# Seven of the first block's eight output-projection units in a seven-product form, behind one plain unit

## The chip, the cores and the metric

The kernel runs on one core of one Trainium2 chip. The metric is the device time of one execution in microseconds (us), lower is better. The engines are TensorE (PE, with its weight loads shown as PEld), VectorE (DVE), ScalarE (ACT), GpSimd (POOL) and the DMA queues, of which SyncE (SP) issues the stream of weights.

## What is computed

Three blocks run one after the other over 256 tokens of width 1024, all in float32. The change is in the end of the first block, a hybrid of retention and a gated linear recurrence:

```python
proj = jnp.einsum('btd,de->bte', xn, w_in)
q, k, v, g_ret, x_lru, g_lru = jnp.split(proj, IN_SPLITS, axis=-1)
q = rotary(q...); k = rotary(k...) * RET_HEAD_DIM ** -0.5
o_ret = group_norm_heads(chunkwise_retention(q, k, v))
y_ret = o_ret * jax.nn.silu(g_ret)
xc = causal_depthwise_conv(x_lru, conv_w, conv_b)
o_lru = rg_lru(xc, gate_a_w, gate_a_b, gate_x_w, gate_x_b, lru_lambda)
y_lru = o_lru * jax.nn.silu(g_lru)
mixed = jnp.concatenate([y_ret, y_lru], axis=-1)      # 256 x 2048
h = h + jnp.einsum('bte,ed->btd', mixed, w_out)       # w_out: 2048 x 1024
return rms_norm(h, norm_out_g)
```

The second block (block attention, convolution, pooling, an FFN) and the third (FFNs, an RWKV mixer, a gated MLP mixer, cross attention) follow; they take its normed output.

## The kernel before

Activations are kept with the width on the 128 partitions and the 256 tokens in the free dimension; a tile of 8 blocks by 256 tokens holds one activation (`c.h`, `c.xn`, `c.work[0]` to `c.work[9]`). All weights come as one stream of 1 MB units. SP loads them in order into a ring of six slots (`c.ring`, the loop at L2909), each as soon as PE has finished the unit that held its slot six units earlier. The plan numbers the units: `b1_gret` and `b1_glru` (the two gates of block one) are units 16 to 23, `b1_out` (the output projection) is 24 to 31, `b2_q` begins at 32.

A plain unit of the output projection (`d_unit`, L302) holds 256 rows of `w_out` against all 1024 columns: 16 matmuls of 128x128 weights by 256 tokens, into the four PSUM banks 4 to 7. Each float32 matmul shows as two records in the trace. `b1_tensor` (L1034 to the end of the function) runs eight of them: units 0 to 3 read `y_ret` from `work[0]` as soon as its pair of blocks is written (`b1_y`), units 4 to 7 read `y_lru` from `work[7]` (`b1_y_lru`). The last unit completes the banks one after the other, and `add_residual` (L474) on DVE adds each to `c.h`, multiplies it by the gain of the next norm (`gain_blocks`) and folds in the squares that ACT makes. PE goes on with `norm_units` of `b2_q`, which takes the gained blocks one by one.

Other parts of the kernel already use a seven-product form of a 2x2 block product (`fast_products`, L593). A unit covers four pairs of blocks; it has 28 matmuls of 128x128 by 128, 56 records. It wants seven left sides, of which three are sums of weights that POOL writes beforehand (`prepare_weights`, L562: four additions over 128x512 for each unit, into one of two or three tiles, the additions of unit z waiting for PE to be done with the unit that had the same tile), and seven right sides, of which four are sums of activations (three DVE instructions for a pair of blocks in the FFN, L782 to L786). Its result comes as products in two banks, which `fast_sum` (L722) puts together: one ACT copy and four DVE additions. `p1` and `p2`, the first two products, need no sum of activations; the third, `p6`, does (`before_t`). In block one the q, k and v projections (`b1_fast`, ten units z = 0 to 9) have this form.

In `b1_vector` DVE is an in-order list. Its last part writes `y_ret` in four steps (`retention_out`, L1177 to L1182), `y_lru` in four (`lru_out`, L1198), and then runs `add_residual`. POOL's list is: the additions of `b1_fast`; the store of the attention bias of block two to DRAM (`bias_rows`, L2958, from eight partitions); a wait for that store and for the last use of the decay table (`b1_prob` 8, L2962); two loads of the skewed bias (L2964, L2965) into `c.table`, wanted by DVE in block two; the load of `mem` into `work[7]`, once `c.h` is complete.

Of the kernel before, what the change touches and what calls it, by code (L numbers as in the profile page):

```python
# [16 lines left out]
ALU = mybir.AluOpType  # L17
# [3 lines left out]
P = 128  # L21
T = 256
C = 1024
KB = C // P
UNITS = 6
# [27 lines left out]
PLAN = plan()  # L53
# [437 lines left out]


FAST = ["b2_ffn", "l0_ffn1", "l0_ffn2", "l1_ffn1", "l1_ffn2"]
FAST_ORDER = ["b1_fast", "b2_ffn", "l0_ffn1", "l0_x", "l0_ffn2", "l1_ffn1", "gm", "l1_x", "l1_ffn2"]
PREPS = 3


def fast_counts():

    unit_of, first_out, out = [], {}, 0  # L500
    first_unit_of = {}
    for name in FAST_ORDER:
        if name == "b1_fast":
            start, units, outs = PLAN["b1_q"][0] + 2, 10, 10
        elif name == "gm":
            start, units, outs = PLAN["gm_v"][0], 22, 18
        elif name in ("l0_x", "l1_x"):
            start, units, outs = PLAN[name + "q"][0] + 2, 6, 6
        else:
            start, units, outs = PLAN[name][0] + 2, 3 * FFI - 2, 2 * (FFI - 1) + 4  # L510
        first_unit_of[name], first_out[name] = len(unit_of), out
        unit_of += range(start, start + units)
        out += outs
    return unit_of, first_unit_of, first_out


FAST_UNIT, FAST_Z, FAST_G = fast_counts()
# [14 lines left out]
    return 2 if z < FAST_Z["b2_ffn"] else PREPS  # L532


def early_tile(c, z):

    if z % 2:
        flat = c.work[4][:, :, :].rearrange("p a b -> p (a b)")[:, 0:1536]
    else:
        flat = c.table[:, :, :].rearrange("p a b -> p (a b)")[:, 1536:3072]  # L540
    return flat.rearrange("p (s k n) -> p s k n", s=3, k=4)
# [247 lines left out]
def fast_residual(c, dve, name, f, scale, gain, ch):  # L789

    S, r = c.S, RESID.index(name)
    if name == "gm_out":
        g = FAST_G["gm"] + 14
    elif f is None:
        g = FAST_G[name[:-1]] + 2
    else:
        g = FAST_G[name] + 2 * (FFI - 1)

    def complete(b):
        if f is None and name != "gm_out":  # L800
            c.wait_done(dve, PLAN[name][0] + b)
        elif f is None:
            c.wait_done(dve, PLAN[name][0] + 2 * b + 1)
        elif b < 3:
            dve.wait_ge(S["bank_complete"], 3 * DPROJ.index(name) + b + 1)
        else:
            c.wait_done(dve, PLAN[name][0] + 3 * FFI - 1)

    for b in range(4):
        out = c.t1[:, b % 2, :]  # L810
        fast_sum(c, dve, g + b, out, lambda: complete(b), ch)
        dve.wait_ge(S["fast_read"], g + b + 1)
# [30 lines left out]
def b1_scalar(c, act):  # L843
# [27 lines left out]
    n0, q0 = PLAN["b1_q"]  # L871
# [40 lines left out]
    for p in range(5):  # L912
# [9 lines left out]
        if p < 4:  # L922
# [2 lines left out]
            act.wait_ge(S["b1_cen"], p + 1)  # L925
            nc.scalar.activation(c.t1[:, 1, :], W[0][:, 2 * p:2 * p + 2, :].rearrange("p a b -> p (a b)"),
                                 ACT.Square).then_inc(S["b1_cen_sq"], 1)
    rms_scalar(c, act, NK["b1_out"], 0)


def b1_tensor(c, pe):
# [100 lines left out]
    gate_unit(7, lambda: means(3))  # L1032
    variances(3)
    n0, _ = PLAN["b1_out"]  # L1034
    for u in range(8):
        pe.wait_ge(S["b1_y"] if u < 4 else S["b1_y_lru"], u % 4 + 1)
        src = W[0] if u < 4 else W[7]
        d_unit(c, pe, n0 + u, lambda k: src[:, 2 * (u % 4) + k, :], u == 0, u == 7,
               before_fourth=(lambda: pe.wait_ge(S["b1_var_read"], 4)) if u == 0 else None)


def b1_vector(c, dve, ch):
# [158 lines left out]
    for p in range(5):  # L1201
        if p < 4:
            for e in range(2):
                hd = 2 * p + e
                dve.wait_ge(S["b1_scores"], hd + 1)
                if hd == 4:
                    dve.wait_ge(S["decay_loaded"], 48)
                if p > 0:
                    dve.wait_ge(S["b1_o"], p)
                v.tensor_tensor(prob[:, e, 0:T + P], c.ps[:, 4 + e, 0:T + P], dec[:, hd, :], ALU.mult)\  # L1210
                    .then_inc(S["b1_prob"], 1)
            recurrence(p)
        gate(2 * p if p < 4 else 7)
        if p < 3:
            gate(2 * p + 1)
        if p < 4:
            dve.wait_ge(S["b1_mean"], p + 1)
            v.tensor_tensor(W[0][:, 2 * p:2 * p + 2, :].rearrange("p a b -> p (a b)"), c.t1[:, 0, :],
                            c.ps[:, 7, :], ALU.subtract).then_inc(S["b1_cen"], 1)
        if p > 0:  # L1220
            retention_out(p - 1)
        if p == 3:
            lru_out(0)
            lru_out(1)
    lru_out(2)
    lru_out(3)
    add_residual(c, dve, "b1_out", PLAN["b1_out"][0] + 7, 1.0, lambda b: ("norm_out_g", b))
    rms_vector(c, dve, "b1_out", c.h)


# [95 lines left out]

def b2_tensor(c, pe):
    S, nc, V, mm = c.S, c.nc, b2_views(c), c.nc.tensor.matmul
    norm_units(c, pe, "b2_q", "b1_out")

    pe.wait_ge(S["rstd_ready"], NK["b1_out"] + 1)
    for name in ("b2_k", "b2_v"):
        n0, q0 = PLAN[name]
        for u in range(2):
            p_unit(c, pe, n0 + u, q0 + u, c.h, token_major=name == "b2_v")
        if name == "b2_k":
            rms_tensor(c, pe, NK["mem"])
# [1552 lines left out]
def build(nc, x, params, consts, late_consts, stream, decay, gates, rel_bias, w_pool, bias_rows, mem, lora1,  # L2890
          lora_wa, lora_g, spatial, spatial_b, out):
    with ExitStack() as ctx:
# [56 lines left out]
        @block.gpsimd  # L2949
        def _(pool):  # L2950
            pool.dma_start(c.relb[0:32, :], rel_bias).then_inc(S["relb_loaded"], 16)
            pool.dma_start(c.wpool[:, :, :], w_pool).then_inc(S["relb_loaded"], 16)

            pool.wait_ge(S["b1_conv"], 6)
            prepare_weights(c, pool, "b1_fast")

            pool.wait_ge(S["b2_bias_read"], 1)
            pool.dma_start(bias_rows.rearrange("h p y -> h p y"),  # L2958
                           c.relg[0:8, :].rearrange("h (a y) -> h a y", a=1).to_broadcast([8, P, 384]))\
                .then_inc(S["bias_loaded"], 16)  # L2960
# [130 lines left out]
```

## Time and profile before

| | before |
|---|---|
| median of 3 runs | 2053.35 us (2051.73 to 2053.61) |
| the profiled execution | 2053.31 us |
| its span | 2051.5 us |
| PE busy | 2017.8 us, 98% of the span |
| PE weight loads busy | 1906.2 us, 93% |
| DVE busy | 1162.4 us, 57% |
| ACT busy | 377.3 us, 18% |
| POOL busy | 1071.3 us, 52% |
| granted TensorE clock, mean | 0.993 |

The span runs from the first to the last instruction; the execution around it adds 1.8 us. Busy time is the union of an engine's instructions. Starts are in us from the start of the span. The granted clock is a share of full speed (1.00 is 2.4 GHz, 0.50 is 1.2 GHz). In a timeline a row merges instructions of one kind that follow each other; "[idle before <-releaser]" stands where the engine had been idle.

### The profile page before, as it was taken

To read this page: it belongs to the slowest core of one execution; us is meant where nothing else is said; L and a number is where in the kernel's file an instruction comes from. 1 tells how busy PE (TensorE), PEld (TensorE's weight loads), DVE (VectorE), ACT (ScalarE), POOL (GpSimd) and SP (SyncE) were. 2 spreads that over 40 slices of the span, in tenths; PEclk is the share of its full clock that TensorE was granted. 3 is DMA by queue.
4 is the path that set the end of the run, shared out by engine and by line. 5 is a ranking of instruction groups with operands and counts; after the bars stand their busy time and mean duration, and the time that the engine had idled before them with its cause. 6 is when DMAs were issued, how large, how long until landed. Compare 5 with 4: busy or idle time off the path is not lost.

```text
span 2051.5 us, 39961 instructions
## 1 busy us (share of the span) xinstructions
PE 2017.8 (98%) x17174; PEld 1906.2 (93%) x17174; DVE 1162.4 (57%) x2002; ACT 377.3 (18%) x787; POOL 1071.3 (52%) x815
## 2 busy tenths in 40 slices
PE   8999999999999999999999999999999999999998
PEld 7998887899998999978788999999999999999998
DVE  6866134456516774436757577726772455576752
ACT  1352022133202000023421210001000231120000
POOL 1820000368853888300001568885888677547884
PEclk9999999999999999999999999999999999999999
DMA  8463443344443444523002344444444544434441
GB/s 313 149 187 138 164 162 114 125 165 168 175 173 123 165 167 172 180 103 123 24 4 103 116 155 173 175 165 164 165 165 166 204 163 147 151 115 167 171 175 64
DMA packets 44025, 307.67 MB, mean 150 GB/s; under 512 B 5304, under 2 KB 5560, under 8 KB 8016
## 3 DMA queue, kind: packets, MB, share of 16 engines
q1 hardware_dynamic: 40752, 291.78, 39.6%
q0 software_dynamic: 2096, 7.31, 1.3%
q10 hardware_dynamic: 1008, 6.10, 0.8%
q8 instruction: 135, 2.21, 0.4%
q14 instruction: 34, 0.28, 0.1%
HBM read 302.54 MB, written 2.62 MB: 149 GB/s over the span
## 4 chain that ended last, share of the span: by engine, by line
PE 91%; DVE 6%; issue 1%; ACT 1%; DMA 0%; DVEq 0%; SPq 0%; ACTq 0%
PE ps L612 60%; PE ps L252 13%; PE ps L311 5%; PE ps L249 2%; PE ps L271 1%; PE ps L286 1%; DVE sb_work L425 1%; PE ps L1730 1%; DVE sb_xn L2667 1%; DVE sb_work L418 1%; PE ps L1755 1%; PE ps L393 0%; DVE sb_h L813 0%; DMA sb_ring<-stream 0%; PE ps L2425 0%
## 5 line engine op out<-in xcount | busy, mean ns | idle before, releaser
L612 PE MATMUL ps<-sb_work,sb_ring 128*128 128x128 f32 x4064 | 487.9, 275 | 0.3 <-DVE sb_work L2049 0.3
L612 PEld LDWEIGHTS ps<-sb_work,sb_ring 128*128 128x128 f32 x4064 | 470.6, 192 | 1.0 <-issue 0.5
L573 POOL TENSOR_TENSOR sb_table<-sb_ring 128x512 f32<-128x512 f32 x131 | 168.2, 1284 | 420.2 <-PE ps L612 196.3
L612 PE MATMUL ps<-sb_work,sb_table 128*128 128x128 f32 x2304 | 291.8, 275 | 0.0
L612 PEld LDWEIGHTS ps<-sb_work,sb_table 128*128 128x128 f32 x2304 | 274.2, 192 | 0.0
L576 POOL TENSOR_TENSOR sb_ring<-sb_ring 128x512 f32<-128x512 f32 x199 | 274.1, 1377 | 0.0
L575 POOL TENSOR_TENSOR sb_table<-sb_table,sb_ring 128x512 f32<-128x512 f32 x131 | 183.9, 1404 | 10.3
L612 PE MATMUL ps<-sb_xn,sb_ring 128*128 128x128 f32 x1536 | 187.3, 275 | 0.0
L612 PEld LDWEIGHTS ps<-sb_xn,sb_ring 128*128 128x128 f32 x1536 | 180.1, 192 | 0.6
L578 POOL TENSOR_TENSOR sb_table<-sb_ring,sb_table 128x512 f32<-128x512 f32 x131 | 175.8, 1342 | 0.0
L573 POOL TENSOR_TENSOR sb_pad<-sb_ring 128x512 f32<-128x512 f32 x63 | 80.6, 1280 | 158.8 <-PE ps L612 111.0
L252 PE MATMUL ps<-sb_work,sb_ring 128*128 128x256 f32 x736 | 162.8, 380 | 0.0
L252 PEld LDWEIGHTS ps<-sb_work,sb_ring 128*128 128x128 f32 x736 | 139.4, 190 | 20.5 <-issue 1.7
L612 PE MATMUL ps<-sb_work,sb_pad 128*128 128x128 f32 x1144 | 144.2, 275 | 0.0
L612 PEld LDWEIGHTS ps<-sb_work,sb_pad 128*128 128x128 f32 x1144 | 135.9, 192 | 0.0
L729 DVE TENSOR_TENSOR sb_t<-ps,sb_std 128x256 f32<-128x256 f32 x75 | 31.3, 417 | 148.1 <-ACT sb_std L683 148.1
L311 PE MATMUL ps<-sb_work,sb_ring 128*128 128x256 f32 x480 | 104.3, 379 | 0.8 <-DVE sb_work L2819 0.8
L311 PEld LDWEIGHTS ps<-sb_work,sb_ring 128*128 128x128 f32 x480 | 91.0, 190 | 14.1 <-DVE sb_work L2819 1.2
L683 ACT ACTIVATE sb_std<-ps 128x128 f32<-128x128 f32 x80 | 22.1, 276 | 417.7 <-PE ps L612 417.7
L575 POOL TENSOR_TENSOR sb_pad<-sb_pad,sb_ring 128x512 f32<-128x512 f32 x63 | 87.1, 1382 | 5.0
L733 DVE TENSOR_TENSOR sb_t<-ps,sb_t 128x256 f32<-128x256 f32 x100 | 42.5, 425 | 82.3 <-PE ps L612 80.5
L729 DVE TENSOR_TENSOR sb_t<-ps,sb_rstd 128x256 f32<-128x256 f32 x25 | 10.5, 422 | 138.6 <-ACT sb_rstd L683 138.6
(454 smaller groups left out, 3113.0 us busy)
## 6 DMA issues: line engine op xcount, KB each, us to landing
sb_ring<-stream SPq DMA_DIRECT2D x275, 1024.0 KB, 4.8
sb_table<-decay ACTq DMA_DIRECT2D x2, 768.0 KB, 21.0
bias_rows<-sb_relg POOLq DMA_DIRECT2D x1, 1536.0 KB, 35.2
sb_con<-consts ACTq DMA_DIRECT2D x1, 1216.0 KB, 9.6
sb_table<-lora POOLq DMA_DIRECT2D x1, 1152.0 KB, 6.0
sb_h<-x SPq DMA_DIRECT2D x2, 512.0 KB, 6.6
sb_ring<-stream SPq DMA_DIRECT2D x2, 512.0 KB, 8.6
sb_work<-gates ACTq DMA_DIRECT2D x1, 1024.0 KB, 14.1
```

Of the source, the lines that this page charges most:

```text
L249: mm = c.nc.tensor.matmul(out[:, m, :], x[:, k, m * P:m * P + P], w[:, k, :], start=k == 0, stop=k == KB - 1)
L252: mm = c.nc.tensor.matmul(out[:, m, :], w[:, k, m * P:m * P + P], x[:, k, :], start=k == 0, stop=k == KB - 1)
L271: mm = c.nc.tensor.matmul(c.bank(q)[:, m * T:m * T + T], w[:, k, m * P:m * P + P], x[:, k, :], start=k == 0 and m == 0, stop=k == KB - 1, ...
L311: mm = c.nc.tensor.matmul(c.ps[:, 4 + m // 2, (m % 2) * T:(m % 2) * T + T], w[:, k, m * P:m * P + P], x2(k), start=first and k == 0 and m ...
L573: v.tensor_tensor(s[:, 0], a[1][0], a[1][1], ALU.add).then_inc(S["fw_ready"], 1)
L575: v.tensor_tensor(s[:, 1], s[:, 0], a[0][0], ALU.subtract).then_inc(S["fw_ready"], 1)
L576: v.tensor_tensor(a[1][0], a[0][0], a[1][0], ALU.subtract).then_inc(S["fw_ready"], 1)
L578: v.tensor_tensor(s[:, 2], a[0][1], s[:, 1], ALU.subtract).then_inc(S["fw_ready"], 1)
L612: ins = mm(fast_bank(c, g, b)[:, i * P:i * P + P], *(sides[::-1] if token_major else sides), start=first and i == 0 and j == 0, stop=last ...
L683: c.nc.scalar.activation(first_product(c, g), fast_bank(c, g, 0)[:, 0:P], ACT.Copy).then_inc(c.S["fast_p1"], 1)
L729: ch.step(v.tensor_tensor(out.rearrange("p (a t) -> p a t", a=4)[:, 0:4:3, :], two[:, P:3 * P].rearrange("p (a t) -> p a t", a=2), p1, ALU ...
L733: ch.step(v.tensor_tensor(out[:, P:3 * P].rearrange("p (a t) -> p a t", a=2), two[:, 4 * P:6 * P].rearrange("p (a t) -> p a t", a=2), u2, ...
```

## The change

Unit 24 stays plain. Units 25 to 31, seven units with 1792 rows of `w_out`, are stored by `fast_d_units` and run by `fast_products`: four parts of the output columns, each over seven pairs of blocks, so that a part takes seven quarters of a unit. The part order uses banks 0 to 3 in turns of two; the plain unit's product stays in banks 4 to 7. PE waits for all four steps of `y_ret` and the first of `y_lru` before it begins, and at the first `p6` for the sums of the first four pairs. DVE gains `spread_out`, three additions for each of seven pairs, all behind `lru_out(3)`; then four additions of the plain unit's banks to `c.h`; then `fast_residual` in place of `add_residual`. POOL gains seven sets of additions (z = 10 to 16, tiles in `work[8]` and `work[1]` in turn): the first ahead of the bias store, the other six behind the two bias loads. PE waits for the third part to be read before `b2_q` and the fourth before `b2_k`. In ACT's list `rms_scalar` is replaced by the same squares with `copy_first` ahead of each.

```diff
-FAST_ORDER = ["b1_fast", "b2_ffn", ...]
+FAST_ORDER = ["b1_fast", "b1_out", "b2_ffn", ...]
+OUT_PAIRS = 7
+OUT_PLAIN = 8 - OUT_PAIRS
...
 def early_tile(c, z):
-    if z % 2:
+    if z >= FAST_Z["b1_out"]:
+        flat = c.work[1 if z % 2 else 8][:, :, :].rearrange("p a b -> p (a b)")[:, 0:1536]
+    elif z % 2:
...
# b1_scalar
-    rms_scalar(c, act, NK["b1_out"], 0)
+    for b in range(4):
+        copy_first(c, act, FAST_G["b1_out"] + b)
+        act.wait_ge(S["h_ready"], b + 1)
+        squares(c, NK["b1_out"], b, c.h)
+    rms_root(c, act, NK["b1_out"])
# b1_tensor
-    for u in range(8):
-        pe.wait_ge(S["b1_y"] if u < 4 else S["b1_y_lru"], u % 4 + 1)
-        src = W[0] if u < 4 else W[7]
-        d_unit(c, pe, n0 + u, lambda k: src[:, 2 * (u % 4) + k, :], u == 0, u == 7,
+    for u in range(OUT_PLAIN):
+        pe.wait_ge(S["b1_y"], u + 1)
+        d_unit(c, pe, n0 + u, lambda k: W[0][:, 2 * u + k, :], u == 0, False,
...
+    pe.wait_ge(S["b1_y"], 4)
+    pe.wait_ge(S["b1_y_lru"], OUT_PLAIN)
+    for u in range(4):
+        c.wait_read(pe, qg + 4 + u)
+    def spread_of(k):
+        return lambda: pe.wait_ge(S["b1_spread"], 4 + 3 * (k + 1))
+    for u in range(OUT_PAIRS):
+        pe.wait_ge(S["fw_ready"], 4 * (z0 + u) + 4)
+        at = 4 * u
+        while at < 4 * u + 4:
+            part = at // OUT_PAIRS
+            pairs = range(at, min(4 * u + 4, OUT_PAIRS * part + OUT_PAIRS))
+            if at % OUT_PAIRS == 0 and part > 1:
+                pe.wait_ge(S["fast_read"], g - 1)
...
+            ins = fast_products(c, pe, n0 + OUT_PLAIN + u, z0 + u, pairs, ...
+                                at % OUT_PAIRS == 0, end, spread_of(pairs[-1]) if part == 0 else None)
...
# b1_vector
+    def spread_out(k):
+        p = k + OUT_PLAIN
+        dve.wait_ge(S["b1_y" if p < 4 else "b1_y_lru"], p % 4 + 1)
+        y4, yt4 = (x.rearrange("p (a t) -> p a t", a=4) for x in (out_pair(c, k), out_spread(c, k)))
+        v.tensor_tensor(yt4[:, 0:2, :], y4[:, 1:4:2, :], y4[:, 0:2, :], ALU.subtract).then_inc(S["b1_spread"], 1)
+        dve.wait_ge(S["b1_spread"], 4 + 3 * k + 1)
+        v.tensor_tensor(yt4[:, 2, :], y4[:, 3, :], yt4[:, 0, :], ALU.subtract).then_inc(S["b1_spread"], 1)
+        dve.wait_ge(S["b1_spread"], 4 + 3 * k + 2)
+        v.tensor_tensor(yt4[:, 3, :], y4[:, 2, :], yt4[:, 2, :], ALU.subtract).then_inc(S["b1_spread"], 1)
     lru_out(2)
     lru_out(3)
-    add_residual(c, dve, "b1_out", PLAN["b1_out"][0] + 7, 1.0, lambda b: ("norm_out_g", b))
+    for k in range(OUT_PAIRS):
+        spread_out(k)
+    c.wait_done(dve, PLAN["b1_out"][0] + OUT_PLAIN - 1)
+    for b in range(4):
+        h = c.h[:, 2 * b:2 * b + 2, :]
+        ch.step(v.tensor_tensor(h, h, c.ps[:, 4 + b, :].rearrange("p (m t) -> p m t", m=2), ALU.add))
+    fast_residual(c, dve, "b1_out", None, 1.0, lambda b: ("norm_out_g", b), ch)
# b2_tensor
+    pe.wait_ge(S["fast_read"], FAST_G["b1_out"] + 3)
     norm_units(c, pe, "b2_q", "b1_out")
     pe.wait_ge(S["rstd_ready"], NK["b1_out"] + 1)
+    pe.wait_ge(S["fast_read"], FAST_G["b1_out"] + 4)
# gpsimd
             prepare_weights(c, pool, "b1_fast")
+            pool.wait_ge(S["b1_m_ready"], 8)
+            prepare_weights(c, pool, "b1_out", slice(0, 1))
             pool.wait_ge(S["b2_bias_read"], 1)
             pool.dma_start(bias_rows..., ...)
...
+            prepare_weights(c, pool, "b1_out", slice(1, None))
             pool.wait_ge(S["h_ready"], HR["b1_out"])
             pool.dma_start(c.work[7][:, :, :], mem).then_inc(S["late_loaded"], 16)
```

## Rows read from the trace of the kernel before

**Rows 1.** The page: chain that ended last, shares of the span by engine.

```profile
PE 91%; DVE 6%; issue 1%; ACT 1%; DMA 0%; DVEq 0%; SPq 0%; ACTq 0%
```

**Rows 2.** Chain that ended last, in order, 180 to 260: start, length, what.

```profile
195.67 0.86 PE ps L1012 x2
196.53 55.25 PE ps L311 x256
251.78 6.91 PE ps L271 x32
```

**Rows 3.** Timeline of PE, `b1_fast`: start, length, line, operands, records.

```profile
54.17 1.95 PE L612 MATMUL ps<-sb_xn,sb_ring 128*128 128x128 f32 x16
...
60.42 1.95 PE L612 MATMUL ps<-sb_xn,sb_ring 128*128 128x128 f32 x16
```

**Rows 4.** Timeline of DVE, last part of block one's list and its residual.

```profile
203.49 0.69 DVE L1182 TENSOR_TENSOR sb_work<-sb_work 128x512 f32<-128x512 f32 x1
204.09 1.28 DVE L1198 SCALAR_TENSOR_TENSOR sb_work<-sb_work 128x512 f32<-128x512 f32 x2
246.64 0.69 DVE L479 SCALAR_TENSOR_TENSOR sb_h<-ps,sb_h 128x512 f32<-128x512 f32 x1 [41.26 <-PE ps L311]
```

**Rows 5.** Timeline of DVE in an FFN, POOL idle: the same three sums, next operation.

```profile
665.28 0.43 DVE L782 TENSOR_TENSOR sb_work<-sb_work 128x256 f32<-128x256 f32 x1
...
666.28 0.42 DVE L729 TENSOR_TENSOR sb_t<-ps,sb_std 128x256 f32<-128x256 f32 x1
```

**Rows 6.** Timeline of DVE in an FFN, POOL at work.

```profile
1423.14 1.38 DVE L782 TENSOR_TENSOR sb_work<-sb_work 128x256 f32<-128x256 f32 x1
...
1425.83 1.38 DVE L786 TENSOR_TENSOR sb_work<-sb_work 128x128 f32<-128x128 f32 x1
```

**Rows 7.** Timeline of POOL beside rows 6: one unit's four additions.

```profile
1419.54 1.28 POOL L573 TENSOR_TENSOR sb_pad<-sb_ring 128x512 f32<-128x512 f32 x1 [1.17 <-PE ps L612]
...
1424.20 1.46 POOL L578 TENSOR_TENSOR sb_pad<-sb_ring,sb_pad 128x512 f32<-128x512 f32 x1
```

**Rows 8.** Timeline of POOL, block one: additions with two tiles, bias store and load.

```profile
60.73 1.27 POOL L573 TENSOR_TENSOR sb_table<-sb_ring 128x512 f32<-128x512 f32 x1 [3.13 <-PE ps L612]
...
64.54 1.72 POOL L578 TENSOR_TENSOR sb_table<-sb_ring,sb_table 128x512 f32<-128x512 f32 x1
...
113.47 1.10 POOL L2958 DMA_DIRECT2D bias_rows<-sb_relg  x1
185.78 0.92 POOL L2964 DMA_DIRECT2D sb_table<-bias_rows  x1 [71.20 <-DVE sb_hid L1210]
186.69 0.89 POOL L2965 DMA_DIRECT2D sb_table<-bias_rows  x1
```

**Rows 9.** Page, DMA issues: KB each, us to landing.

```profile
sb_ring<-stream SPq DMA_DIRECT2D x275, 1024.0 KB, 4.8
...
bias_rows<-sb_relg POOLq DMA_DIRECT2D x1, 1536.0 KB, 35.2
```

**Rows 10.** DMA queue q0 in 128 to 131: packets, MB, share of 16 engines.

```profile
q0 software_dynamic: 33, 0.15, 48.0%
```

**Rows 11.** The same in 137 to 140.

```profile
q0 software_dynamic: 33, 0.15, 20.9%
```

**Rows 12.** Timeline of SP: the load of unit 25 (`b1_out`'s second).

```profile
157.37 0.33 SPq L2913 DMA_DIRECT2D sb_ring<-stream  x1
```

**Rows 13.** Timeline of PE, 150 to 200: unit 20, and the next product of probabilities.

```profile
160.52 7.07 PE L252 MATMUL ps<-sb_xn,sb_ring 128*128 128x256 f32 x32
...
175.19 0.59 PE L997 MATMUL ps<-sb_hid,sb_work 128*128 128x256 f32 x2
```

**Rows 14.** By stretch: length, busy of PE, PEld, DVE, ACT, POOL, then granted clock.

```profile
980.00:982.00 2.00, 0.00 (x0) 0.00 (x0) 1.97 (x6) 0.00 (x0) 0.00 (x0) 0.95 0.00 0
982.00:984.00 2.00, 1.77 (x7) 1.40 (x8) 1.28 (x3) 1.68 (x3) 1.24 (x1) 0.50 0.00 0
...
988.00:990.00 2.00, 2.00 (x66) 1.55 (x66) 1.61 (x3) 0.60 (x1) 0.00 (x0) 0.84 0.00 0
```

More of the change, by code:

```diff
@@ L493 @@
 FAST = ["b2_ffn", "l0_ffn1", "l0_ffn2", "l1_ffn1", "l1_ffn2"]
-FAST_ORDER = ["b1_fast", "b2_ffn", "l0_ffn1", "l0_x", "l0_ffn2", "l1_ffn1", "gm", "l1_x", "l1_ffn2"]
+FAST_ORDER = ["b1_fast", "b1_out", "b2_ffn", "l0_ffn1", "l0_x", "l0_ffn2", "l1_ffn1", "gm", "l1_x", "l1_ffn2"]
 PREPS = 3
+OUT_PAIRS = 7
+OUT_PLAIN = 8 - OUT_PAIRS
 def fast_counts():
@@ L504, in fast_counts @@
             start, units, outs = PLAN["b1_q"][0] + 2, 10, 10
+        elif name == "b1_out":
+            start, units, outs = PLAN[name][0] + OUT_PLAIN, OUT_PAIRS, 4
         elif name == "gm":
@@ L532, in tiles, with out_pair, out_spread @@
     return 2 if z < FAST_Z["b2_ffn"] else PREPS
+def out_pair(c, k):
+    p = k + OUT_PLAIN
+    return c.work[0 if p < 4 else 7][:, 2 * (p % 4):2 * (p % 4) + 2, :].rearrange("p j t -> p (j t)")
+def out_spread(c, k):
+    p = k + OUT_PLAIN
+    return c.work[3 if p < 4 else 4][:, 2 * (p % 4):2 * (p % 4) + 2, :].rearrange("p j t -> p (j t)")
 def early_tile(c, z):
-    if z % 2:
+    if z >= FAST_Z["b1_out"]:
+        flat = c.work[1 if z % 2 else 8][:, :, :].rearrange("p a b -> p (a b)")[:, 0:1536]
+    elif z % 2:
         flat = c.work[4][:, :, :].rearrange("p a b -> p (a b)")[:, 0:1536]
@@ L793, in fast_residual @@
         g = FAST_G["gm"] + 14
+    elif name == "b1_out":
+        g = FAST_G[name]
     elif f is None:
@@ L799, in complete @@
     def complete(b):
-        if f is None and name != "gm_out":
+        if name == "b1_out":
+            if b < 3:
+                dve.wait_ge(S["bank_complete"], 3 * DPROJ.index(name) + b + 1)
+            else:
+                c.wait_done(dve, PLAN[name][0] + 7)
+        elif f is None and name != "gm_out":
             c.wait_done(dve, PLAN[name][0] + b)
@@ L1034, in b1_tensor @@
     n0, _ = PLAN["b1_out"]
-    for u in range(8):
-        pe.wait_ge(S["b1_y"] if u < 4 else S["b1_y_lru"], u % 4 + 1)
-        src = W[0] if u < 4 else W[7]
-        d_unit(c, pe, n0 + u, lambda k: src[:, 2 * (u % 4) + k, :], u == 0, u == 7,
+    for u in range(OUT_PLAIN):
+        pe.wait_ge(S["b1_y"], u + 1)
+        d_unit(c, pe, n0 + u, lambda k: W[0][:, 2 * u + k, :], u == 0, False,
                before_fourth=(lambda: pe.wait_ge(S["b1_var_read"], 4)) if u == 0 else None)
+    z0, g = FAST_Z["b1_out"], FAST_G["b1_out"]
+    pe.wait_ge(S["b1_y"], 4)
[12 more added lines that the diff above has]
+                pe.wait_ge(S["fast_read"], g - 1)
+            if u == 1 and part == 0:
+                pe.wait_ge(S["b1_y_lru"], 4)
+            end = pairs[-1] % OUT_PAIRS == OUT_PAIRS - 1
+            ins = fast_products(c, pe, n0 + OUT_PLAIN + u, z0 + u, pairs,
+                                lambda k, j, t: out_pair(c, k % OUT_PAIRS)[:, j * T + t * P:j * T + t * P + P],
+                                lambda k, m: out_spread(c, k % OUT_PAIRS)[:, m * P:m * P + P], g,
+                                at % OUT_PAIRS == 0, end, spread_of(pairs[-1]) if part == 0 else None)
+            if end and part < 3:
+                ins.then_inc(S["bank_complete"], 1)
+            g += end
+            at = pairs[-1] + 1
+        ins.then_inc(S[f"unit_done{(n0 + OUT_PLAIN + u) % UNITS}"], 1)
 def b1_vector(c, dve, ch):
@@ L1224, in b1_vector @@
             lru_out(1)
+    def spread_out(k):
+        p = k + OUT_PLAIN
+        dve.wait_ge(S["b1_y" if p < 4 else "b1_y_lru"], p % 4 + 1)
[5 more added lines that the diff above has]
+        v.tensor_tensor(yt4[:, 3, :], y4[:, 2, :], yt4[:, 2, :], ALU.subtract).then_inc(S["b1_spread"], 1)
     lru_out(2)
     lru_out(3)
-    add_residual(c, dve, "b1_out", PLAN["b1_out"][0] + 7, 1.0, lambda b: ("norm_out_g", b))
+    for k in range(OUT_PAIRS):
[5 more added lines that the diff above has]
+    fast_residual(c, dve, "b1_out", None, 1.0, lambda b: ("norm_out_g", b), ch)
     rms_vector(c, dve, "b1_out", c.h)
@@ L3038 @@
         units += p_units(cut[i])
-    units += d_units(a["w_out"])
+    units += d_units(a["w_out"][:256 * OUT_PLAIN]) + fast_d_units(a["w_out"][256 * OUT_PLAIN:])
     w2 = a["w_in_2"][0]
```

## The prediction

> **What bounds the kernel now.** I read the page first: PE makes 91% of the chain that ended last [rows 1]. So PE's time counts, and every gap put into PE is paid in full. Next the chain in order of time around the first block's output projection: it is one piece of PE work, 256 records in 55.25 us, with PE work right before and right behind it [rows 2]. A unit of 32 records takes 55.25 / 8 = 6.91 us and there is no gap to win; a change here wins only what it takes off PE's own work. Then DVE's list at that place: y_ret is complete at 203.49 + 0.69 = 204.18 and y_lru at 204.09 + 1.28 = 205.37, after which DVE idles 41.26 us for the banks [rows 4]. These times matter now, because today PE needs the late pairs only unit by unit, up to 48 us later, while the changed PE needs several of them at once. Last I read POOL's list, since POOL gets work on which PE will wait.
>
> **PE's own work.** In the seven-product form a unit takes 60.42 - 54.17 = 6.25 us [rows 3], 0.1116 us for each of its 56 records, at full clock. Seven units win 7 x (6.91 - 6.25) = 4.6 us. This is all the change can give: 0.22% of the time.
>
> **The wait for y.** The plain unit ends at 196.53 + 6.91 = 203.44. The fast units begin once y_ret is complete, about 204.25 with a semaphore's delay: 0.8 us.
>
> **The wait for the sums.** In the first fast unit p1 and p2 of four pairs, 16 records, take 1.8 us: PE stands before p6 at about 206.0. It now wants the sums of four pairs, all behind lru_out(3) in DVE's list, that is behind 205.37. A pair takes 666.28 - 665.28 = 1.0 us when POOL is idle [rows 5], so four pairs would be ready at 209.4, a pause of 3.4 us. When POOL works, the same three instructions take 1425.83 + 1.38 - 1423.14 = 4.1 us a pair [rows 6]: each is stretched to about the length of one POOL addition. So the question is what POOL does from 203 to 210. The Trainium skill (GPSIMD Engine Reference, Specifications) says that GpSimd shares its SBUF interfaces with VectorE and contends with instructions that have two SBUF inputs. By that rule the sums suffer and the additions from PSUM do not; rows 5 and 6 agree for the sums.
>
> **Where POOL is.** Its first new set, z = 10, waits for unit 25, which SP issues at 157.37 [rows 12] and which lands 4.8 us later [rows 9], at 162.2. The set takes 5.5 us (60.73 to 64.54 + 1.72) [rows 8] up to 6.1 us beside a busy DVE (1419.54 to 1424.20 + 1.46) [rows 7], so it ends near 168. Only then is the bias store issued, 54 us later than today's 113.47 [rows 8]. It took 35.2 us to land [rows 9]. I do not expect it to be faster where fewer other transfers run: in two stretches of 3 us it moved the same 0.15 MB, one with next to nothing beside it and one with two other queues active [rows 10, 11]; 1.5 MB at 0.05 MB/us is some 30 us and its start is slower. So it lands between 201 and 203.5, POOL issues the two bias loads (0.92 + 0.89 us, rows 8) and starts z = 11 at 203 to 205.3, exactly on DVE's sums. For some 6 us DVE gets about one instruction in 1.35 us: 4 to 5 of them, which lose 0.65 us each if they are of 0.69 us and 1.0 us each if they are sums. That is 3.3 us, taken between 2.8 and 4.1. The sums of four pairs are ready at 209.4 + 3.3 = 212.7. The pause before p6 is 6.7 us. The bias itself is wanted only in block two; the store's later place costs nothing else. The ring loads that run beside it arrive later, but unit 26 is issued when unit 20 is done, 160.52 + 7.07 = 167.6, and wanted at 204. DVE's instructions of 162 to 168 lose up to 3 us to z = 10 as well; what hides that is gate work on PE, which takes up the probabilities again at 175.19 [rows 13].
>
> **POOL's pace afterwards.** With two tiles z waits for PE to be done with z - 2: 0.3 us plus 5.5 to 6.1 us of additions against 6.25 us of PE work [rows 3, 7, 8]. z = 11 is ready at 209 to 211.4 and wanted at 212.7 + 40 x 0.1116 = 217.2. The others fit or miss by up to 0.2 us. I take 0.2 us for the five, between 0 and 1.0.
>
> **The clock.** PE stands for nearly 7 us. In the RWKV mixer PE did nothing in 980 to 982; the granted clock fell inside that gap to 0.50 (1.2 GHz) and was back at full level within 988 to 990, some 6.8 us at half (a mean of 0.95 over 2 us is 0.2 us at half, a mean of 0.84 is 0.6 us, and the 6 us between were at 0.50) [rows 14]. If the fall comes between 2 and 6 us into the pause and lasts as long, 2 to 6 us of PE work run at half level: a loss of 1 to 3 us, and I take 2. It could be nothing (the gap there followed a stretch of small matmuls, this one follows dense ones) or the whole 3.4 us. The Trainium skill (TensorE: Matmul & The Clock Gate, HAM oscillation) warns against idle gaps between matmul bursts because the engine falls to its low level in them; by its rule this term is certain, and rows 14 agree for a gap of 2.2 us.
>
> **The end of the stage.** The last part's residual is longer (four DVE sums before the addition to h, of the size of the one of 0.42 us in rows 5), an estimated 1 to 1.5 us more between the last product and the folded squares. PE runs a whole unit of b2_q in that time, 6.91 us [rows 2], needs the last gained blocks only in its last quarter, and the squares after it. POOL's last set is done by then. The unit hides it; without b2_q's cover it would be that 1 to 1.5 us. The four additions of the plain unit (0.7 us each by L479, rows 4) stand behind the sums and before the first part is complete at about 222: price 0. The waits for `fast_read` before b2_q and b2_k ask for parts finished 10.9 us and 14 us earlier: price 0. The load of mem moves with h, about 1 us later against PE; its norm is wanted 20 us later.
>
> **The sum.** -4.6 + 0.8 + 6.7 + 0.2 + 2.0 = +5.1 us. The profiled execution (2053.31) and the median (2053.35) agree, so the forecast is 2053.35 + 5.1 = 2058.4 us, with its own range from 2056.3 (no clock loss, small contention) to 2061.
>
> **The rivals.** A measurement of this kernel can tell about 0.2% from no change, 4.1 us: 2049.2 to 2057.5 counts as the same.
> *The sums meet no POOL work.* The place is DVE's sums at 205 to 209; it decides if the store lands before about 196 or if the stretching is not what rows 6 say. Then the pause is 3.4 us: -4.6 + 0.8 + 3.4 + 0.2 = -0.2, and 0 to 2 us of clock: 2053.1 to 2055.2. For it: the store's start was slow today while it shared the queues; against it: the constant rate of rows 10 and 11. Chance 0.22.
> *The contention comes, but the clock stays.* -4.6 + 0.8 + 6.7 + 0.2 = +3.1: 2056.4. Chance 0.12.
> *POOL becomes the bound.* If the store lands later than about 209, z = 11 is late too, and sets that take 6.1 us plus a longer hand-over than 0.3 us pace PE: 6.7 us a unit instead of 6.25 over five units and a late start of 2 us give 5.1 + 2.3 + 2 = +9.4 us: 2062.8. For it: ring loads and store collide, and both run beside the gates. Against: slack of 6 us at z = 11. Chance 0.11.
> *The gain survives.* The sums are ready before PE asks, as if DVE were ahead by 3 us; the time is 2053.35 - 4.6 + 0.8 = 2049.5, or 2048.8 without the wait for y. Nothing in DVE's list speaks for it: its last steps hang on PE's own L1012 at 195.67 [rows 2]. Chance 0.05.
> The forecast keeps 0.50.
>
> **How the numbers follow.** Slower by over 0.2%: four fifths of 0.50, all of 0.11, a quarter of 0.12 and a little of the first rival make 0.56. Faster by over 0.2%: most of the last rival, 0.04. The same: 0.40. The range leaves out the last rival, the lowest part of the first and the upper end of the third: 2053.4 to 2062.5.
>
> **What would show it.** In the profile after: the granted clock below 1 just behind 206; a PE idle of about 6.7 us before a product of L612, released by DVE, near 213; DVE's new sums at 1.2 to 1.4 us each while POOL's second new set stands beside them, and 0.3 to 0.45 afterwards; the bias store near 168 and its landing near 203; seven units of 6.25 us; b2_q's first product about 5 us later than 251.78. The prediction is wrong if the store lands early, if the sums run at 1.0 us a pair, or if PE waits for POOL again and again.

## The result

| | before | after |
|---|---|---|
| median of 8 runs | 2052.18 us (2049.82 to 2054.04) | 2058.77 us (2055.83 to 2060.54) |
| ratio | | 1.0035, 95% interval 1.0026 to 1.0044 |
| the profiled execution | 2053.31 us | 2058.39 us |
| its span | 2051.5 us | 2056.5 us |
| granted TensorE clock, mean | 0.993 | 0.994 |
| from the first product of the output projection to the first of `b2_q` | 55.25 us | 61.79 us |

The changed kernel is slower by 0.35%, 6.6 us between the medians, and the stage alone is 6.54 us longer. From the page of the kernel after, the busy time of each engine:

```profile
PE 2012.8 (98%) x17342; PEld 1906.1 (93%) x17342; DVE 1189.9 (58%) x2043; ACT 378.4 (18%) x791; POOL 1109.4 (54%) x843
```

PE is less busy by 5 us and the time is longer: PE stands where it never stood. The timeline of PE in that stage (start, length, line, operands, records, then the idle before) answers to [rows 2, 3]:

```profile
197.03 7.07 PE L311 MATMUL ps<-sb_work,sb_ring 128*128 128x256 f32 x32
204.89 2.05 PE L630 MATMUL ps<-sb_work,sb_ring 128*128 128x128 f32 x16 [0.79 <-DVE sb_work L1239]
215.13 4.55 PE L630 MATMUL ps<-sb_work 128*128 128x128 f32 x24 [8.19 <-DVE sb_work L1290]
219.51 3.29 PE L630 MATMUL ps<-sb_work,sb_ring 128*128 128x128 f32 x28
...
258.82 7.07 PE L271 MATMUL ps<-sb_work,sb_ring 128*128 128x256 f32 x32
```

The plain unit, the short wait for y_ret, the 16 records of p1 and p2, then 8.19 us of nothing until VectorE's twelfth sum (L1290). The records behind it are slow: the first 24 take 4.55 us where 2.84 is usual. VectorE in the same stretch, which answers to [rows 4 to 6]:

```profile
204.15 0.69 DVE L1239 TENSOR_TENSOR sb_work<-sb_work 128x512 f32<-128x512 f32 x1
204.75 3.43 DVE L1255 SCALAR_TENSOR_TENSOR sb_work<-sb_work 128x512 f32<-128x512 f32 x2
208.10 1.48 DVE L1286 TENSOR_TENSOR sb_work<-sb_work 128x256 f32<-128x256 f32 x1
209.62 1.23 DVE L1288 TENSOR_TENSOR sb_work<-sb_work 128x128 f32<-128x128 f32 x1
210.88 1.23 DVE L1290 TENSOR_TENSOR sb_work<-sb_work 128x128 f32<-128x128 f32 x1
212.04 0.41 DVE L1286 TENSOR_TENSOR sb_work<-sb_work 128x256 f32<-128x256 f32 x1
...
214.78 0.29 DVE L1290 TENSOR_TENSOR sb_work<-sb_work 128x128 f32<-128x128 f32 x1
```

And GpSimd, which answers to [rows 8]:

```profile
162.92 1.27 POOL L591 TENSOR_TENSOR sb_work<-sb_ring 128x512 f32<-128x512 f32 x1 [48.73 <-DMA sb_ring<-stream]
...
168.84 1.10 POOL L3035 DMA_DIRECT2D bias_rows<-sb_relg  x1
204.14 0.92 POOL L3041 DMA_DIRECT2D sb_table<-bias_rows  x1 [34.20 <-DMA bias_rows<-sb_relg]
205.05 0.90 POOL L3042 DMA_DIRECT2D sb_table<-bias_rows  x1
205.96 1.66 POOL L591 TENSOR_TENSOR sb_work<-sb_ring 128x512 f32<-128x512 f32 x1
...
210.66 1.30 POOL L596 TENSOR_TENSOR sb_work<-sb_ring,sb_work 128x512 f32<-128x512 f32 x1
221.61 1.26 POOL L591 TENSOR_TENSOR sb_work<-sb_ring 128x512 f32<-128x512 f32 x1 [9.64 <-PE ps L630]
```

The reader sees the chain whole: the store goes out behind z = 10 at 168.84, POOL waits 34.20 us for it, issues the bias loads, and its additions for z = 11 fill 205.96 to 211.96. VectorE's five instructions in that time (two of `lru_out`, three sums) take 1.2 to 1.75 us each; POOL is done at 211.96, and the next sum, begun at 212.04, takes 0.41 us again and the ones behind it 0.3 to 0.4. The first `lru_out` (204.75 to 206.50) would alone have ended at 205.44, 0.5 us before POOL's first recorded addition, and is stretched as well; this is open, see the run with the sums early. Last the clock, by stretch of 2 us (length; busy of PE, PEld, DVE, ACT, POOL; granted clock; DMA share, GB/s), which answers to [rows 14]:

```profile
208.00:210.00 2.00, 0.00 (x0) 0.00 (x0) 1.97 (x3) 0.00 (x0) 2.00 (x2) 1.00 0.98 406
210.00:212.00 2.00, 0.00 (x0) 0.00 (x0) 1.97 (x2) 0.00 (x0) 1.97 (x2) 0.92 1.03 408
...
216.00:218.00 2.00, 2.00 (x11) 2.00 (x11) 1.86 (x8) 0.00 (x0) 0.00 (x0) 0.50 0.00 0
218.00:220.00 2.00, 2.00 (x18) 2.00 (x17) 1.93 (x4) 0.00 (x0) 0.00 (x0) 0.87 0.00 0
```

A mean of 0.92 over 2 us is 0.3 us at half, so the clock fell to 0.50 (1.2 GHz) at 211.7, 5.0 us into the pause, and stayed there for some 3.4 us of work behind it.

The stage is 6.54 us longer and begins 0.66 us later, as the whole first block of this profile does from its first unit on; yet the profiled execution is only 5.1 us longer. The rest lies later: in 1055 to 1085, the RWKV mixer, the profile of the kernel before has a fall of the clock that the profile after has not. None of the nine other profiles below has it either, and one of them is the kernel before with a single wait added, so it is not the change that took it away. The same columns, before:

```profile
1055.00:1085.00 30.00, 27.06 (x701) 25.15 (x694) 12.19 (x17) 10.72 (x18) 0.00 (x0) 0.89 0.02 3
```

and after:

```profile
1055.00:1085.00 30.00, 28.61 (x849) 27.02 (x846) 10.81 (x16) 10.32 (x18) 0.00 (x0) 1.00 0.01 4
```

One profiled execution against another is therefore good to 2 or 3 us for the whole, but far better for one stage. The experiments below are read by the stage, from the first product of L311 to the first of L271, in one profile of each kernel; the ratios are from 6 to 12 executions of each variant.

### The profile page after: what moved, and what is told of

The parts are those of the page before. It is cut to its first block, busy times and chain, and to the rows that moved or that the text cites. A ratio compares the mean times of both kernels' runs of the same rounds, so it can differ in the third digit from the quotient of the medians.

```text
span 2056.5 us, 40380 instructions
## 1 busy us (share of the span) xinstructions
PE 2012.8 (98%) x17342; PEld 1906.1 (93%) x17342; DVE 1189.9 (58%) x2043; ACT 378.4 (18%) x791; POOL 1109.4 (54%) x843
## 4 chain that ended last, share of the span: by engine, by line
PE 90%; DVE 7%; issue 1%; ACT 1%; DMA 0%; DVEq 0%; SPq 0%; ACTq 0%
PE ps L630 62%; PE ps L252 13%; PE ps L311 2%; PE ps L249 2%; PE ps L271 1%; PE ps L286 1%; DVE sb_work L425 1%; PE ps L1805 1%; DVE sb_xn L2742 1%; DVE sb_work L418 1%; PE ps L1830 1%; PE ps L393 0%; DVE sb_h L838 0%; DMA sb_ring<-stream 0%; PE ps L2307 0%
## 5 line engine op out<-in xcount | busy, mean ns | idle before, releaser
L630 PE MATMUL ps<-sb_work,sb_ring 128*128 128x128 f32 x4288 | 514.8, 275 | 1.1 <-DVE sb_work L1239 0.8
L630 PEld LDWEIGHTS ps<-sb_work,sb_ring 128*128 128x128 f32 x4288 | 496.5, 192 | 2.2 <-DVE sb_work L1239 1.2
L594 POOL TENSOR_TENSOR sb_ring<-sb_ring 128x512 f32<-128x512 f32 x206 | 284.4, 1381 | 0.0
L630 PEld LDWEIGHTS ps<-sb_xn,sb_ring 128*128 128x128 f32 x1536 | 180.1, 192 | 0.6
L252 PE MATMUL ps<-sb_work,sb_ring 128*128 128x256 f32 x736 | 162.8, 380 | 0.0
L252 PEld LDWEIGHTS ps<-sb_work,sb_ring 128*128 128x128 f32 x736 | 139.4, 190 | 20.5 <-issue 1.7
L252 PEld LDWEIGHTS ps<-sb_xn,sb_ring 128*128 128x128 f32 x384 | 72.7, 190 | 13.0 <-issue 3.5
L252 PE MATMUL ps<-sb_xn,sb_ring 128*128 128x256 f32 x384 | 84.6, 379 | 0.0
```

The lines of the kernel that those rows point to most:

```text
L252: mm = c.nc.tensor.matmul(out[:, m, :], w[:, k, m * P:m * P + P], x[:, k, :], start=k == 0, stop=k == KB - 1)
L594: v.tensor_tensor(a[1][0], a[0][0], a[1][0], ALU.subtract).then_inc(S["fw_ready"], 1)
L630: ins = mm(fast_bank(c, g, b)[:, i * P:i * P + P], *(sides[::-1] if token_major else sides), start=first and i == 0 and j == 0, stop=last ...
```

## The experiments

The theory: the pause comes from VectorE's sums, 4 us of it from their place in VectorE's order and the rest from z = 11 beside them, and z = 11 is there because the bias store was put behind z = 10; the clock adds 2 us. Rivals: the sums are slow for another reason (the transfers), the slow records behind the pause are a cost of the restart, GpSimd's pace bounds the units, the late store costs something by itself.

| kernel | stage, us | pause before p6 | ratio to before, 95% interval |
|---|---|---|---|
| before | 55.25 | none | 1 |
| the change | 61.79 | 8.19 | 1.0035 (1.0026 to 1.0044) |
| store first | 56.72 | 3.10 | 1.0000 (0.9986 to 1.0014) |
| the change, PE kept busy | 60.10 | 0.51 | 1.0022 (1.0010 to 1.0035) |
| z = 11 behind the sums | 57.27 | 3.11 | 1.0020 (1.0010 to 1.0031) |
| sums early, store late | 60.78 | 5.93 | 1.0037 (1.0023 to 1.0050) |
| two plain units, store late | 54.40 | none (2.80 later) | 1.0002 (0.9992 to 1.0012) |
| two plain units, store first | 51.33 | none | 0.9983 (0.9973 to 0.9993) |
| sums early, store first | 52.94 | 0.91 | 0.9990 (0.9980 to 0.9999) |
| store first, PE kept busy | 55.11 | 0.42 | 1.0004 (0.9994 to 1.0013) |
| before, store late | 55.25 | none | 0.9996 (0.9986 to 1.0005) |

**The store first.**

```diff
             pool.wait_ge(S["b1_conv"], 6)
             prepare_weights(c, pool, "b1_fast")
-            pool.wait_ge(S["b1_m_ready"], 8)
-            prepare_weights(c, pool, "b1_out", slice(0, 1))
             pool.wait_ge(S["b2_bias_read"], 1)
             pool.dma_start(bias_rows..., ...)
+            pool.wait_ge(S["b1_m_ready"], 8)
+            prepare_weights(c, pool, "b1_out", slice(0, 1))
             pool.wait_ge(S["bias_loaded"], 16)
             pool.wait_ge(S["b1_prob"], 8)
```

> The changed kernel with one thing moved on GpSimd: the bias store goes back ahead of the first new set of weight sums (z = 10), so it is issued near 114 instead of 168.8 and has landed near 149. Theory: the second set (z = 11) then starts at about 188, when the decay table is free, and ends near 194, so VectorE's twelve sums meet no GpSimd work: 1.0 us a pair, the sums of four pairs ready 4.0 us after lru_out(3), TensorE's pause before the first p6 3.5 to 4.0 us instead of 8.2; with the clock term gone or halved the stage is 4.3 to 6 us shorter than in the changed kernel (61.8 us), so the time is about 2052 to 2054 and no longer slower than before by 0.2%. Rival (the sums are slow by themselves, or the late store matters only through the loads behind it): the pause stays at 7 us or more and the time within 1 us of the changed kernel's.

GpSimd's second new set and its third:

```profile
186.51 1.57 POOL L591 TENSOR_TENSOR sb_work<-sb_ring 128x512 f32<-128x512 f32 x1
...
214.43 1.27 POOL L591 TENSOR_TENSOR sb_work<-sb_ring 128x512 f32<-128x512 f32 x1 [22.54 <-PE ps L630]
```

and PE:

```profile
202.77 2.05 PE L630 MATMUL ps<-sb_work,sb_ring 128*128 128x128 f32 x16 [0.79 <-DVE sb_work L1239]
207.92 4.29 PE L630 MATMUL ps<-sb_work 128*128 128x128 f32 x24 [3.10 <-DVE sb_work L1290]
```

z = 11 runs at 186.5, the pause is 3.10 us and the stage is 5.1 us shorter. Between this and the change lie only lines of GpSimd: 5.1 us of the 6.54 come from where the store stands. Whether by GpSimd's additions or by the transfers beside them, the next run tells. The two `lru_out` took 1.28 us and each pair's sums 1.0 us, so the sums are not slow by themselves. The time is that of the kernel before. The clock fell here too, and behind the pause, which had ended at 207.92:

```profile
208.00:210.00 2.00, 2.00 (x15) 2.00 (x16) 1.86 (x7) 0.00 (x0) 0.00 (x0) 0.82 0.00 0
210.00:212.00 2.00, 2.00 (x11) 2.00 (x10) 1.90 (x5) 0.00 (x0) 0.00 (x0) 0.50 0.00 0
212.00:214.00 2.00, 2.00 (x16) 2.00 (x16) 1.52 (x3) 0.00 (x0) 0.00 (x0) 0.83 0.03 8
```

That is 0.7 + 2 + 0.7 = 3.4 us at half, from 209.3.

**z = 11 behind the sums.** The late store stays and the contention goes by one wait:

```diff
+            pool.wait_ge(S["b1_spread"], 4 + 3 * 4)
             prepare_weights(c, pool, "b1_out", slice(1, None))
```

> The changed kernel, store late as it is, with one wait added: GpSimd starts z = 11 only when the sums of four pairs are written. This takes the contention away without touching the store. Theory: the sums are ready 4.0 us after lru_out(3), near 210; the pause is 3.1 to 3.5 us and the clock falls as in the run with the store first; z = 11 runs from 210 to 216 while z = 10's unit ends near 216 too with the slower clock, so TensorE waits for GpSimd by 0 to 1 us once. Stage 56.7 to 57.8 us against 61.8. Rival (the sums' slowness comes from the transfers that run at the same time: ring loads and bias loads had the DMA engines near full in 206 to 212): the sums stay at 1.2 us or more each and the stage above 60 us.

VectorE at the end of the fourth pair's sums and behind it, and GpSimd's start:

```profile
206.57 0.29 DVE L1288 TENSOR_TENSOR sb_work<-sb_work 128x128 f32<-128x128 f32 x1
206.90 0.29 DVE L1290 TENSOR_TENSOR sb_work<-sb_work 128x128 f32<-128x128 f32 x1
207.11 0.42 DVE L1286 TENSOR_TENSOR sb_work<-sb_work 128x256 f32<-128x256 f32 x1
207.56 1.24 DVE L1288 TENSOR_TENSOR sb_work<-sb_work 128x128 f32<-128x128 f32 x1
```

```profile
207.28 1.38 POOL L591 TENSOR_TENSOR sb_work<-sb_ring 128x512 f32<-128x512 f32 x1 [4.16 <-DVE sb_work L1290]
```

```profile
206.00:208.00 2.00, 0.76 (x6) 0.76 (x7) 1.90 (x6) 0.00 (x0) 0.72 (x1) 1.00 1.02 412
```

In 206 to 208 the DMA engines are full (share 1.02, 412 GB/s) and the sums take 0.29 and 0.42 us until GpSimd begins at 207.28; the next one takes 1.24. The transfers are not the cause, GpSimd at work is. Instructions with an input in PSUM do not suffer: the four additions of the plain unit's banks, one input in PSUM, took 2.84 us beside GpSimd here and 2.84 with GpSimd idle in the change. The price: its set then ends later, and VectorE's sums for pairs 5 to 7 are stretched instead, 0.27 us of which PE sees. The stage fell by 4.5 us against the change.

**Is it the clock or the restart?** 34 products of 128x128 by 128 into an idle bank before the wait at the first p6, results unused:

```diff
     def spread_of(k):
-        return lambda: pe.wait_ge(S["b1_spread"], 4 + 3 * (k + 1))
+        def before():
+            if k == 3:
+                for _ in range(34):
+                    nc.tensor.matmul(c.ps[:, 2, 0:P], c.c("ident"), c.xn[:, 0, 0:P], start=True, stop=True)
+            pe.wait_ge(S["b1_spread"], 4 + 3 * (k + 1))
+        return before
```

> The changed kernel with 34 added matmuls of 128x128 by 128 (68 records, 7.6 us) into an unused bank while TensorE waits for the first four pairs' sums; their results are not used. They fit in the 8.2 us of the pause. Theory: the granted clock stays at 1.00 throughout, the records behind the wait run at 0.1116 us from the start, and the stage is 1.8 us shorter (61.8 to 60.0 us), all of it behind the wait; the wait itself still ends with VectorE's twelfth sum at the same place. Rival (the slow records behind the wait are a weight-load or semaphore effect of the restart, not the clock): the stage keeps 61.8 us although the clock shows 1.00.

```profile
206.61 7.76 PE L1078 MATMUL ps<-sb_xn,sb_con 128*128 128x128 f32 x68
214.88 2.94 PE L630 MATMUL ps<-sb_work 128*128 128x128 f32 x24 [0.51 <-DVE sb_work L1295]
```

With something to do PE kept its clock (1.00 in every stretch from 206 to 224), the first 24 records took 2.94 us instead of 4.55, and the stage was 1.69 us shorter with the wait ending on the same sum. The slow records were not a cost of the restart. The same edit with 12 products in the kernel with the store first:

> The changed kernel with the store first (pause 3.1 us, clock at half for about 3.9 us of work right after it, stage 56.7 us) with 12 added matmuls (24 records, 2.7 us) in the pause, results unused. Theory: the granted clock stays at 1.00 and the stage falls by 1.9 us to 54.8 us. Rival (a pause this short is not what makes the clock fall; something else at that place does): the clock still falls near 209 and the stage stays near 56.7 us.

Clock at 1.00 throughout, stage 55.11 instead of 56.72: 1.6 us. The clock's price is shown twice. (The expectation's 3.9 us at half is 3.4 by the stretches above.) When the clock falls is not settled by these: it fell with pauses of 3.10, 3.11, 5.93 and 8.19 us, in the first two only behind the pause, and stayed with 0.91 and 2.80 us. In [rows 14] it fell in a gap of 2.2 us among small products, so the length of the pause alone does not decide.

**The sums early, the store late.** VectorE does the first pair's sums before the last mean and the next three behind `retention_out(3)`, ahead of `lru_out(2)` and `lru_out(3)`:

```diff
+        if p == 3:
+            spread_out(0)
...
+    for k in range(1, 4):
+        spread_out(k)
     lru_out(2)
     lru_out(3)
-    for k in range(OUT_PAIRS):
+    for k in range(4, OUT_PAIRS):
         spread_out(k)
```

> The changed kernel, store late as it is, with VectorE's order changed: the sums of the first pair go into its idle time before the last mean, those of the next three right behind retention_out(3), ahead of lru_out(2) and lru_out(3). Theory: nine sums instead of fourteen instructions stand between the last y_ret and p6. Free they would be ready 3.0 us after 204.9, at 207.9, a pause of 1.0 us; z = 11 begins at 206.0 and stretches what is left by then, some five sums by 1.0 us each: ready near 211 to 212, pause 4 to 5 us, clock loss about 2 us, stage 57.5 to 58.8 us. Rival (the order does not matter, only GpSimd's end at 212 does): the sums are ready when GpSimd ends plus 1 us, near 213, stage 60 us.

The stage was 60.78 us, and the rival was nearer. Free, the nine sums would have been done near 207.7; with z = 11 beside them (206.35 to 211.8) they were done at 212.71, 0.9 us after GpSimd's end. Five of them were stretched, by 1.0 us each, as the theory had it: 207.7 + 5.0 = 212.7, and the 211 to 212 that it forecast had added less than its own count. Five instructions fewer stood in the way and it won 2.3 us of pause (8.19 to 5.93), of which the clock took back 1.24 (44.93 us from the first p6 to `b2_q` against 43.69): the fall came late in the pause and lay on 6 us of work,

```profile
212.77 5.49 PE L630 MATMUL ps<-sb_work 128*128 128x128 f32 x24 [5.93 <-DVE sb_work L1266]
218.05 3.64 PE L630 MATMUL ps<-sb_work,sb_ring 128*128 128x128 f32 x28
```

One sum, of 1.38 us from 205.10, should have ended 1.0 us before GpSimd's first recorded addition (206.35) and is stretched all the same, while GpSimd issues the second bias load; the first `lru_out` of the change is like it. In the run with z = 11 behind the sums, VectorE's instructions beside both issues were not stretched. This stays open; GpSimd's times are rough.

With the store first the same order of VectorE gives what it should:

> Seven units in the new form, the store ahead of z = 10, and VectorE's order with the first pair's sums in its idle time and the next three right behind retention_out(3). Theory: no contention, three pairs' sums behind the last y_ret, so the pause before p6 is 3.0 + 0.1 us less the 1.8 us of p1 and p2, that is 1.1 to 1.3 us; stage 55.25 - 4.6 + 0.8 + 1.2 = 52.7 us if the clock stays, 54.6 us if it falls as after the 3.1 us pause. It would still lie above the 51.3 us of two plain units with the store first. Rival (the sums put ahead of the last mean delay the second chain through VectorE and y is late too): the wait for y grows by 1 us or more.

Pause 0.91 us, clock at 1.00, stage 52.94 us. The first pair's sums met z = 11 at 189 to 192.2 and took 3.3 us there, in time that VectorE idled in the kernel with the store first (3.1 us before its next step); y was not late, the wait for it 0.82 us against 0.79.

**Two plain units.**

```diff
-OUT_PAIRS = 7
+OUT_PAIRS = 6
...
```

The lines left out are waits: two parts now end with a unit, and their end is told by the unit's own semaphore.

> The changed kernel with one size changed: OUT_PAIRS = 6, two plain units ahead of six in seven-product form (two parts now end with a unit, so their end is told by the unit's own semaphore). Theory: TensorE has 6.9 us more to do while VectorE works, y is complete before it asks, and the contention stays where it is, so the pause before p6 falls from 8.2 us to about 2.1 us (8.2 + 0.8 - 6.9), and the work is 0.66 us longer than with seven. The run with the store first lost 1.9 us to the clock with a pause of 3.1 us, so this term is open here: stage 55.25 - 3.9 + 2.1 = 53.4 us without it, 55.3 us with it. Rival (GpSimd's pace bounds the fast units, or the pause does not depend on what TensorE has to do meanwhile): 57 us or more.

The stage, 54.40 us, is 1.0 us above the forecast without a clock loss, and not for the reason given: the contention did not stay where it was. No pause came before p6 at all, and one of 2.80 us came later, for GpSimd:

```profile
214.58 1.95 PE L630 MATMUL ps<-sb_work,sb_ring 128*128 128x128 f32 x16
219.33 1.16 PE L630 MATMUL ps<-sb_work,sb_ring 128*128 128x128 f32 x8 [2.80 <-POOL sb_work L596]
```

```profile
172.60 1.26 POOL L591 TENSOR_TENSOR sb_work<-sb_ring 128x512 f32<-128x512 f32 x1 [59.14 <-DMA sb_ring<-stream]
...
177.61 1.10 POOL L3035 DMA_DIRECT2D bias_rows<-sb_relg  x1
212.38 0.92 POOL L3041 DMA_DIRECT2D sb_table<-bias_rows  x1 [33.67 <-DMA bias_rows<-sb_relg]
```

With two plain units the first set belongs to unit 26, which is loaded 10 us after unit 25; the store moved with it to 177.61, landed at 212, and z = 11 came too late for PE instead of on the sums. The late store is the root in both cases; it only hits another place. Both edits together, two plain units and the store first:

> Two plain units and the store ahead of z = 10. Theory: no contention with the sums (ready about 208 to 210) and p6 reached only near 212, so no pause, no clock loss: stage 55.25 - 6 x 0.66 = 51.3 us, 3.9 us below the kernel before; time ratio about 0.998. If GpSimd's pace matters it shows as short waits of TensorE for it ahead of single units, up to 1 us in all: 52.3 us. Rival (the seven-product units cost something beside the pause, such as a longer tail into block two): stage as forecast, but the following stages up to the first FFN start less than 3 us earlier.

This is the theory without any of its faults: no idle of PE in the whole stage, 51.33 us, 3.92 below the kernel before, against 6 x 0.66 = 3.9. `b2_q` begins 6.38 us earlier in its profile than in that of before (245.24 against 251.62), 2.46 of it from a first block that began earlier and 3.92 from the stage; a table load of ACT well into the second block is also 6.38 us earlier (377.40 against 383.78), so the longer tail costs nothing. In the change the same two places are both 7.2 us later. It has the lowest median of all, 2047.06 us, and is clear of both kernels.

**The late store alone, in the kernel before.** GpSimd waits for unit 26 ahead of the store:

```diff
             pool.wait_ge(S["b2_bias_read"], 1)
+            c.wait_loaded(pool, PLAN["b1_out"][0] + 2)
             pool.dma_start(bias_rows..., ...)
```

> The kernel before with the bias store alone put late: GpSimd waits for unit 26 of the stream to be loaded before it issues the store, so it is issued near 172 instead of 113.5. Nothing of the new form is in it. Theory (the store's later place costs nothing by itself; its price in the changed kernel is only that it puts z = 11 on the sums): the stage stays 55.25 us, the time within 0.1% of the kernel before, and the store lands 34 to 35 us after its issue as it does at 113 and at 168. Rival (ring loads beside the store, or the late bias, hold up block two): waits for the ring or the bias appear between 200 and 300 and the time is more than 2 us longer.

```profile
174.28 1.10 POOL L2959 DMA_DIRECT2D bias_rows<-sb_relg  x1 [59.71 <-DMA sb_ring<-stream]
209.27 0.92 POOL L2965 DMA_DIRECT2D sb_table<-bias_rows  x1 [33.89 <-DMA bias_rows<-sb_relg]
```

The stage stays 55.25 us and PE waits for nothing between 120 and 300, nor does it in the kernel before. The store's place costs nothing by itself.

## Why the prediction was right, and where it was off

The forecast was 2058.4 us, +5.1; measured 2058.77, +6.6 between the medians and +6.54 in the stage. Term by term, with the after profile's stage split at its starts (197.03 + 6.91 = 203.94, 204.89, 204.89 + 1.79 = 206.68, 215.13, 258.82):

| term | forecast | measured |
|---|---|---|
| PE's own work | -4.6 | 6.91 + 392 x 0.1116 - 55.25 = -4.6 (with six units and no pause the stage fell by 3.92 against 3.9) |
| wait for y | +0.8 | 204.89 - 203.94 = +0.95 (see below) |
| pause before p6 | +6.7 | 215.13 - 206.68 = +8.45 |
| GpSimd's pace | +0.2 | 0 (no wait of PE for POOL) |
| clock and restart | +2.0 | 43.69 - 376 x 0.1116 = +1.7 (1.6 and 1.7 less with PE kept busy, in two kernels) |
| end of the stage | 0 | 0 (7.2 us late at `b2_q` and still 7.2 at ACT's table load of 383.78) |
| sum | +5.1 | +6.5 |

**Right.** The place of the store (168 forecast, 168.84), its time to landing whatever runs beside it (35.0 at 168.84, 34.7 at 174, 35.2 to 35.5 between 111 and 113.5), z = 11 on top of the sums, the fall of the clock inside the pause (5.0 us into it, within the 2 to 6 us of the term, though not "just behind 206"), the free tail. That the median came within 0.4 us of the forecast is in part luck: the stage lost 1.4 us more than forecast, and the kernel before has a median 1.2 us lower over eight runs (2052.18) than over the three that the forecast stood on (2053.35).

**Mis-sized: the step that says what DVE loses in those 6 us.** It took 4 to 5 instructions at 0.65 us for the long ones and 1.0 for the sums, 3.3 us. That is the sum for four; for five, two long ones and three sums, the same prices give 4.3 us, above its own upper end of 4.1. There were five, and the long ones lost more: the two `lru_out` took 3.43 us against 1.28 in the kernel with the store first, 1.07 each, and the three sums 212.04 - 208.10 = 3.94 against 1.0, 0.98 each: 5.1 us. I had read the stretched length off short instructions only (1.25 to 1.38 us, rows 6) and put the long ones at the same length; they take 1.75. The profile of the kernel before had such a row, right ahead of rows 6:

```profile
1421.47 1.64 DVE L778 SCALAR_TENSOR_TENSOR sb_work<-sb_t,sb_hid 128x512 f32<-128x512 f32 x1
```

Rows like it that lie wholly beside additions take 1.64 to 1.76 us, against 0.69 alone. And z = 11 began at 205.96. Less the 0.66 us by which this profile's first block lies later, that is 205.3, the late end of 203 to 205.3. With 5.1 the pause would have been forecast at 8.5.

**The wait for y** is 0.15 us longer than forecast by a reading: 196.53, the start of the plain unit in the chain of [rows 2], is not on the scale of the timelines, where the same product begins at 196.37, and y's 204.18 was taken from a timeline.

**The clock term** was right in size, but by its own reasoning it could as well have been 3: from the first p6 to `b2_q` it took 42.08 us with PE kept busy, 43.69 here and 44.93 with the sums early, that is 1.6 and 2.9 us of clock, since it depends on when in the pause the fall comes. The verdict, slower by over 0.2%, rested on the contention: without it the change is level (1.0000), with it but without the clock's fall it is at 1.0022 (1.0010 to 1.0035), just at the mark.

**The rivals.** "The sums meet no POOL work" put the time at 2053.1 to 2055.2, -0.2 plus up to 2 of clock; made real, it gave +1.5 us in the stage. "POOL becomes the bound" did not happen here; with two plain units and the late store its first half did, z = 11 too late for PE, once and for 2.80 us, and the sets behind it kept up. "The contention comes, but the clock stays" put it at +3.1; with PE kept busy the stage was +4.85, above it by the mis-sized pause.

## What to carry to other kernels

When a wait is added to an in-order list, follow what is queued behind the thing it waits behind: here a set of additions put ahead of a slow store moved 34 us of waiting, and everything queued behind it, onto the one place where another engine was on PE's path. Before a form that wants data earlier replaces one that takes it piece by piece, lay the producer's list against the moment of need: seven of eight units saved 4.6 us and paid 8.5 us of pause, six of eight with the store first saved 3.9 and paid nothing. The four pauses in PE of 3.10 to 8.19 us before the first p6 also cost 1.6 to 2.9 us of half clock each, so such a pause counts for more than its length. And before a price is read off rows, look for a row of the size that will pay it: the long instructions' 1.64 us stood beside the rows used.

## What was not expected of the hardware

A DVE instruction with two SBUF inputs beside GpSimd's additions of 128x512 was stretched to 1.2 to 1.5 us if it takes 0.3 to 0.4 us alone, and to 1.75 if it takes 0.69: a loss of about 1 us an instruction, whatever its size. It was not so every time: with the sums early one sum begun at 207.71 together with an addition took its 0.41 us, and with PE kept busy one `lru_out` (205.19) took 2.71 us. The bias store, 1.5 MB from eight partitions, took 34.5 to 35.5 us in all eleven profiles, issued between 111 and 178, whatever else was being transferred. The clock fell with pauses of 3.10 us and more in this stage and not with one of 2.80 us, but also in the 2.2 us gap of [rows 14].
